# Empty buffers between the operands: the distance of streamed operands to the weights in on-chip memory is changed

## The reference, cut to what matters

```python
h = _modulate(xl, shift, scale)        # root-mean-square norm, scale and shift
z = h @ w_in                           # (512 x 1024) @ (1024 x many columns)
y = (gelu(conv(g)) * val) @ w_out
xl = xl + gate * y
```

## Time and profile before

| | |
|---|---|
| median of 2 runs | 3673.74 us (3673.59 to 3673.9) |
| profiled execution | 3674.51 us |
| its span, first to last instruction | 3672.7 us |
| mean granted clock of TensorE | 0.995 |
| instructions | 56,483, of them 21,302 matmuls and as many weight loads |

### The profile page before, as it was taken

The page is one execution under the profiler, slowest core; times in us unless marked ns, Lnnn a source line. Parts: engine busy times, 40 slices in busy tenths (PEclk is TensorE's granted clock), DMA queues, the critical chain, the costliest instruction groups (busy, mean ns, idle before and its releaser), DMA issues.

```text
span 3672.7 us, 56483 instructions
## 1 busy us (share of the span) xinstructions
PE 3572.8 (97%) x21302; PEld 2938.1 (80%) x21302; DVE 1983.1 (54%) x3008; ACT 1620.1 (44%) x2819; POOL 1325.2 (36%) x614
## 2 busy tenths in 40 slices
PE   7999999999999999999999999999999999999998
PEld 5875788888877777888777778789977777878997
DVE  4857553333357775343555653557555665356555
ACT  4344432221266663332655552445455555335444
POOL 2530333232331113444422334355543233344555
PEclk9999999999999999999999999999999999999999
DMA  5368221111220002322312222232322222222332
GB/s 211 115 230 309 92 75 63 63 63 63 69 81 24 24 24 91 99 97 92 102 59 70 70 70 94 77 105 87 115 87 69 70 70 70 86 93 75 110 104 92
DMA packets 85382, 335.84 MB, mean 91 GB/s; under 512 B 9648, under 2 KB 9776, under 8 KB 78640
## 3 DMA queue, kind: packets, MB, share of 16 engines
q1 hardware_dynamic: 84448, 330.79, 26.7%
q10 hardware_dynamic: 720, 2.10, 0.2%
HBM read 329.18 MB, written 2.10 MB: 90 GB/s over the span
## 4 chain that ended last, share of the span: by engine, by line
issue 44%; PE 36%; POOL 14%; DVE 3%; ACT 1%; POOLq 0%; DMA 0%; ACTq 0%; DVEq 0%; SPq 0%
POOL w_lo L3550 14%; PE pB L287 7%; PE pB L288 7%; PE pB L289 6%; PE pT L1095 2%; PE pT L1096 1%; PE pT L1097 1%; PE pT L289 1%; PE pT L288 1%; PE pT L287 1%; PE pO L287 1%; PE pO L289 1%; PE pO L288 1%; PE pO L1097 1%; PE pO L1095 1%
## 5 line engine op out<-in xcount | busy, mean ns | idle before, releaser
L3550 POOL TENSOR_TENSOR w_lo<-w_raw,w_hi 128x1024 fp32r<-128x1024 f32 x452 | 1106.9, 2452 | 2071.2 <-ACT w_hi L333 2070.1
L333 ACT ACTIVATE w_hi<-w_raw 128x1024 fp32r<-128x1024 f32 x452 | 476.5, 1055 | 561.0 <-PE pB L289 365.0
L287 PE MATMUL pB<-h_hi,w_hi 128*128 128x512 f32 x1540 | 607.7, 395 | 18.7 <-DVE h_lo L477 6.0
L288 PE MATMUL pB<-h_lo,w_hi 128*128 128x512 f32 x1540 | 600.3, 390 | 0.0
L289 PE MATMUL pB<-h_hi,w_lo 128*128 128x512 f32 x1540 | 599.5, 389 | 0.0
L287 PE MATMUL pB<-b_hi,w_hi 128*128 128x512 f32 (+1 forms) x1084 | 399.2, 368 | 3.6 <-DVE b_lo L1307 1.6
L288 PE MATMUL pB<-b_lo,w_hi 128*128 128x512 f32 (+1 forms) x1084 | 394.9, 364 | 0.0
L289 PE MATMUL pB<-b_hi,w_lo 128*128 128x512 f32 (+1 forms) x1084 | 394.6, 364 | 0.0
L287 PEld LDWEIGHTS pB<-h_hi,w_hi 128*128 128x128 f32 x1540 | 290.0, 188 | 94.4 <-issue 15.5
L289 PEld LDWEIGHTS pB<-h_hi,w_lo 128*128 128x128 f32 x1540 | 289.8, 188 | 61.0
L288 PEld LDWEIGHTS pB<-h_lo,w_hi 128*128 128x128 f32 x1540 | 290.1, 188 | 58.0 <-issue 1.2
(11 more groups left out here) (673 smaller groups left out, 7085.1 us busy)
## 6 DMA issues: line engine op xcount, KB each, us to landing
w_raw<-stream SPq DMA_DIRECT2D x520, 512.0 KB, 3.3
under<-ada SPq DMA_DIRECT2D x42, 1024.0 KB, 5.6
arena<-ada SPq DMA_DIRECT2D x6, 1024.0 KB, 17.4
x<-xT SPq DMA_DIRECT2D x1, 2048.0 KB, 9.2
out<-x SPq DMA_DIRECT2D x8, 256.0 KB, 2.1
xc<-cT SPq DMA_DIRECT2D x1, 1024.0 KB, 26.5
arena<-bmask ACTq DMA_DIRECT2D x1, 1024.0 KB, 4.9
w_hi<-arena SPq DMA_DIRECT2D x4, 192.0 KB, 8.4
```

The lines of the kernel that those rows point to most:

```text
L287: pe.matmul(dst, lh, rh, start=(begin and k == 0), stop=False)
L288: pe.matmul(dst, lh, rl, start=False, stop=False)
L333: act.activation(w_hi[:, s, :], w_raw[:, s, :], ACT.Copy).then_inc(hi_ready, 1)
L3550: pool.tensor_tensor(w_lo[:, s, :], w_raw[:, s, :], w_hi[:, s, :].bitcast(F32), ALU.subtract).then_inc(lo_ready, 1)
```

## The change

Nine buffers that nothing reads or writes are put between the others: 768 bytes ahead of h_hi, 64 bytes behind each of h_hi, h_lo and b_hi, 1,024 bytes behind b_lo and so ahead of w_raw, 576 bytes ahead of the arena, and 64 bytes behind each of xh_hi, xh_lo and xb_hi. (A buffer of [P, 16] is 64 bytes in each partition, one of [P, 192] 768 bytes.) `under` gets 64 bytes more for each of its four parts, so that they still lie on h_hi, h_lo, b_hi and b_lo. Two slices that ran to the end of such a part now name the end. No instruction is added, removed or moved.

```diff
+        sb("place_h", [P, 192])
-        with nc.sbuf_tensor("under", [P, 4, KD * T], F32) as under:
+        with nc.sbuf_tensor("under", [P, 4, KD * T + 16], F32) as under:
             pass
-        h_hi, h_lo = sb("h_hi", [P, KD * T], F32R), sb("h_lo", [P, KD * T], F32R)
-        b_hi, b_lo = sb("b_hi", [P, KD * T], F32R), sb("b_lo", [P, KD * T], F32R)
+        h_hi, _ = sb("h_hi", [P, KD * T], F32R), sb("place_h_lo", [P, 16])
+        h_lo, _ = sb("h_lo", [P, KD * T], F32R), sb("place_b_hi", [P, 16])
+        b_hi, _ = sb("b_hi", [P, KD * T], F32R), sb("place_b_lo", [P, 16])
+        b_lo, _ = sb("b_lo", [P, KD * T], F32R), sb("place_w", [P, 256])
         w_raw = sb("w_raw", [P, SLOTS + 1, KD * P])
@@
+        sb("place_arena", [P, 144])
         with nc.sbuf_tensor("arena", [P, ARENA], F32) as arena:
@@
-        xh_hi, xh_lo = sb("xh_hi", [P, KD * C], F32R), sb("xh_lo", [P, KD * C], F32R)
-        xb_hi, xb_lo = sb("xb_hi", [P, KD * C], F32R), sb("xb_lo", [P, KD * C], F32R)
-        sb("arena_rest", [P, ARENA - 4 * KD * C])
+        xh_hi, _ = sb("xh_hi", [P, KD * C], F32R), sb("place_xh_lo", [P, 16])
+        xh_lo, _ = sb("xh_lo", [P, KD * C], F32R), sb("place_xb_hi", [P, 16])
+        xb_hi, _ = sb("xb_hi", [P, KD * C], F32R), sb("place_xb_lo", [P, 16])
+        xb_lo = sb("xb_lo", [P, KD * C], F32R)
+        sb("arena_rest", [P, ARENA - 4 * KD * C - 48])
@@
-        spare = [under[:, 1, 0:half], under[:, 2, half:], under[:, 3, half:]]
+        spare = [under[:, 1, 0:half], under[:, 2, half:KD * T], under[:, 3, half:KD * T]]
```

## The result

The changed kernel takes 3713.87 us (median of 2 runs, 3710.23 to 3717.51) against 3673.74: ratio 1.011, 95% interval 1.008 to 1.014. It is slower by 40 us. That is inside 2%, but outside the predicted range of 3590 to 3710 us and 59 us above the forecast.

What follows compares the result with a forecast made beforehand. The prediction took TensorE's matmul stream to bound the kernel. Gains of 14.4 us at 256 columns, 0 at 512 and 4 us for settling sooner summed to 18 us, from 3673.74 to 3655 us, range 3590 to 3710.

Steps and rivals of the forecast that it cites:

- What bounds the kernel: Whole kernel: TensorE, busy 97% of 3672.7 us, sets the end nearly everywhere; time between matmul starts is what matters.
- The distance sets the pitch: Matmuls at 256 columns: streamed operand's address minus the weights' makes the pitch 113.3 ns (distance 192) against 120 (0).
- Modulo 512: All matmuls: distance counted modulo 512 bytes, putting h_hi, h_lo, b_hi, b_lo at 320, 384, 448 and 0.
- The stated doubt about parts at equal distance: Test of the modulo 512 rule: it is wrong if parts at equal distance show different pitches.
- The 512-column matmuls: I take 0: 9,480 matmuls at 512 columns: no change, between bounds of 63 us gain and 57 us loss.
- wherever it lies: 512-column stream: it loses one cycle in 16 at any distance, since 226.7 ns is just twice 113.3.
- 5 ns for 2,872 matmuls at 256 columns, 14.4 us: 256-column matmuls whose distance leaves 0 by more than 64: 5 ns less each, 14.4 us in all.
- nearer to 0: 256-column matmuls on xh_hi and xc_t, 1,112 at distance 64: left at 120 ns, without gain.
- Settling sooner: 512-column matmuls: they settle sooner after each start, 4 us less.
- The 512-column stream no longer settles: Rival, 512-column matmuls: stream stays at 232 ns, 57 us come and 14 go, 3717 us; chance 0.18.
- Gain at 512 too: Rival, 512-column matmuls: 6.7 ns less off distance 0, 90 us with 256 columns, 3584 us, or about 3610; chance 0.25.
- Nothing: Rival, whole kernel: buffer order or neighbours in time, not addresses, make the pitch difference; 3674 us, chance 0.12.

Runs made afterwards that it cites:

- the controls: Against the kernel before: everything from h_hi on 768 bytes further, 3673.44 us against 3673.43; all nine gaps made multiples of 256 bytes, 3673.81 us against 3672.5.

## Why the prediction was wrong, point by point

**What bounds the kernel.** Right. PE's busy time took up all of the change (36.1 of 35.7 us) and no other engine moved. Reading the pitch from starts was right too: the duration of the 512-column group rose by 7 ns (395 to 402 on L293) where h_hi's pitch rose by 4.7 over all its matmuls.

**The distance sets the pitch.** Called an inference, now shown: operands and weights moved together, by 768 or by 64 bytes, keep the 512-column pitch, moving w_lo alone costs 25 us, and `xc_t` brought to 192 reaches 113.6 ns.

**"Modulo 512".** Wrong. The period is 256: h at 256 has 228.0 ns and the groups of before. The stated doubt about parts at equal distance was the right test. What was called 320, 384 and 448 is 64, 128 and 192. This bears on the 256-column sum: by the prediction's own rule (no gain at 64) h_hi drops out of it, and xb_lo, at 256, is at 0 as before. These two make 816 + 176 of its 2,872 matmuls. It also makes b_hi and xb_hi (both 192) the ones with most to gain.

**"The 512-column matmuls: I take 0".** This is the step that failed, and with it the forecast. The term was put at nothing and measured +44 us. Two arguments carried the zero. The first, loads of 188 ns beside 512 columns, said that the load has room; but after the change the loads still take 188 to 189 ns while h_hi's and b_hi's pitch is up by 5, so at 512 columns the load's duration didn't tell the pitch. The second, that 226.7 is twice 113.3 and so a loss "wherever it lies", took a coincidence of two numbers for a law: at distance 192, where 256 columns do reach 113.3, 512 columns have 233.3. The trace of before had no 512-column matmul off distance 0, and both bounds (63 us of gain, 57 of loss) stood in the text; no row spoke for the zero between them more than for either bound. What rows did show is that the kernel has an unsettled state of 232 at exactly the distance that settles best, so a settled 226.7 was something that could be lost.

**5 ns for 2,872 matmuls at 256 columns, 14.4 us.** Right in sign, twice too large: about 7 us. Part of that is the count. It has h_hi and xb_lo in it, as just said, and 256 matmuls on b_lo, which the prediction itself puts back on 0; without these three 1,624 are left, and 8 us. That this comes so near to the measured sum is in part luck, for the 5 ns don't hold either. They came from `attP_t`, whose three matmuls share one distance. With hi and lo parts apart only xh_lo gained that much (119.9 to 115.0); h_lo gained 3.1 ns, xb_hi 2.9, b_hi 1.9, h_hi and xh_hi 0.5. That 64 is "nearer to 0" was no guide either: `xc_t` went to 117.8.

**"Settling sooner", 4 us.** Wrong in sign. In the changed kernel the 512-column steps never come down.

**The rivals.** "The 512-column stream no longer settles" is what happened: 57 in, 14 out, 3717 us, by the mechanism named (each matmul changes the pattern). Measured are 44 in and 7 out, with a median of 3713.87. Both of its terms were too large, and the errors offset each other. The argument against it, that `attP_t` settles at 192, carried a reading at 256 columns over to 512. Half of that rival was incomplete, too: with all parts at one distance of 64 the loss is still 24 us, so it isn't only the stagger. "Gain at 512 too" is ruled out: none of the distances in the table has at 512 columns a pitch below that of distance 0. "Nothing" is ruled out by the controls.

The Trainium skill (SBUF — State Buffer, section "SBUF: two separate sides", and TensorE: Matmul & The Clock Gate, Part 2), as the prediction reads it, would have the sum at 0. These runs differ: with engines, transfers and instructions unchanged, addresses alone moved the 512-column pitch from 227 to between 229 and 236 ns. The 216 ns that the Trainium skill gives for 512 columns (TensorE: Matmul & The Clock Gate, "Back-to-back issue gap") appeared in no run on these operands: the lowest settled pitch is 226.7.

**The chances.** What happened had been given 0.18. The range ended at 3710, 7 us short of the rival's own value; that value was worked out from rows and belonged inside.

## What to carry to other kernels

Where a kernel is bound by matmuls each with a load of its own, compare starts in the timeline with the columns over the clock. Before moving a buffer, look at the addresses of the streamed operand and the weights modulo 256 bytes. In this kernel 512 columns wanted distance 0 for all the parts that follow each other, and 256 columns wanted 192 (worth 2 to 6 ns, by the layout); gaps in multiples of 256 bytes cost nothing. Measure it anew in another kernel. And where one row shows a loss and its condition occurs nowhere else in the trace, its price for the larger class is unknown in sign: run the one kernel that puts that class off the condition before trusting a factor of two.

## What the runs showed of the hardware that was not expected

- The address of the streamed operand relative to the weights, modulo 256 bytes, changes the pitch of matmuls of 128 x 128 weights in this type at the full clock: at 512 columns 226.7 (distance 0, settled), 229.0 or 233.3 (64, settled), a mean of 233.3 (192); at 256 columns 120.0 (0) and, in most layouts, 113.3 to 115.1 (192), though 117.7 in one.
- Neighbours count: with w_lo moved by 64 bytes the first matmul of each three, itself and its successor at distance 0, went from 227.3 to 228.8 ns; with the parts staggered h_hi at 0 went to 232.0.
- At one distance of 64 there are two stable patterns, 229.0 and 233.3 ns, and a gap of 0.75 us was enough to change from one to the other. Whether this is why the times of the kernel at 64 spread over 9 us (3694.46 to 3703.28) isn't shown: only one of its executions has a trace, and the kernel before, whose trace has just one settled pattern, spreads as much (3667.67 to 3677.07).
- A second matmul narrowed to 64 weight columns, its load shortened from 188 to 135 ns, made the kernel slower by 20 us at distance 0 and faster by 11 us at distance 64 (one run each).

What stays open: what inside the chip has the period of 256 bytes; how much of the 13.3 ns at 512 columns belongs to the load, since shortening it changes the matmul and the pattern as well; and why the context's parts at 192 settled at 117.7 ns in one layout and near 115 or 113.3 in two others. No run here tells these apart.
